# One core, a hybrid decoder trunk: attention values half a product later, one output block summed from PSUM, mixers shifted, and the recurrence's scores for half of the columns

## What is computed

```
mod = silu(c) @ w_ada + b_ada;  shift, scale, gate = split(mod)
h = rmsnorm(x, g_pre) * (1 + scale) + shift
p = h @ w_in                                   # 2048 x 1024 @ 1024 x 8704
y_pool = pool_mixer(a_in) * silu(a_g)
y_hgrn = hgrn2_mixer(b_q, b_f, b_i) * silu(b_g)   # gated linear recurrence, 4 heads of 64
y_conv = short_conv_mixer(c_x, c_b, c_c) * silu(c_g)
y_diff = diff_attention(d_q, d_k, d_v) * silu(d_g)  # a = softmax 0 - lambda * softmax 1, causal
merged = sum of sigmoid(m_g[branch]) * (y_branch @ w_merge[branch])
x + gate * rmsnorm(merged @ w_out, g_post)
```

## Time and profile before

| | us |
|---|---|
| median of 3 runs | 2758.57 |
| lowest, highest | 2758.25, 2764.52 |
| the profiled execution, as timed | 2759.86 |
| its span in the trace | 2757.8 |

### The profile page before, as it was taken

How to read it: one execution, slowest core, us unless ns; L and a number is a source line. 1 busy time by engine, 2 the same in 40 slices (tenths; PEclk the granted TensorE clock), 3 DMA queues, 4 the chain that set the end, 5 groups by cost and what they waited for, 6 DMA issues and landing times. The chain is left out here.

```text
span 2757.8 us, 35490 instructions
## 1 busy us (share of the span) xinstructions
PE 2355.1 (85%) x11572; PEld 1913.1 (69%) x11572; DVE 1773.7 (64%) x2868; ACT 1240.0 (45%) x2613; POOL 1231.3 (45%) x1015
## 2 busy tenths in 40 slices
PE   3698868778988889996899999998898965798898
PEld 3576656667776678785787777777677754677676
DVE  6775554544989896544777776688899734453442
ACT  3553444434443444543565656553444333243342
POOL 1442322222866665532333433465767605352543
PEclk9899988989999999998999999999999987899999
DMA  5357533323434334545342332143333356485772
GB/s 209 111 186 228 145 105 90 102 72 116 126 101 122 103 97 128 174 132 151 83 119 77 98 96 83 60 134 117 107 110 123 96 171 159 120 231 143 193 198 73
DMA packets 327262, 350.84 MB, mean 127 GB/s; under 512 B 26416, under 2 KB 244912, under 8 KB 326064
## 3 DMA queue, kind: packets, MB, share of 16 engines
q1 hardware_dynamic: 327088, 348.67, 42.8%
HBM read 242.15 MB, written 106.43 MB: 126 GB/s over the span
## 5 line engine op out<-in xcount | busy, mean ns | idle before, releaser
L1603 PE MATMUL gb<-h_hi,w_hi 128*128 128x512 f32 x1904 | 804.2, 422 | 83.7 <-DVE o L1199 53.4
L1604 PE MATMUL gb<-h_lo,w_hi 128*128 128x512 f32 x1904 | 766.9, 403 | 0.0
L1605 PE MATMUL gb<-h_hi,w_lo 128*128 128x512 f32 x1904 | 766.5, 403 | 0.0
L1191 DVE TENSOR_TENSOR w_lo<-w,w_hi 128x512 fp32r<-128x512 f32 x340 | 333.8, 984 | 337.3 <-ACT w_hi L900 336.5
L1603 PEld LDWEIGHTS gb<-h_hi,w_hi 128*128 128x128 f32 x1904 | 375.0, 197 | 173.7 <-issue 95.9
L1605 PEld LDWEIGHTS gb<-h_hi,w_lo 128*128 128x128 f32 x1904 | 372.4, 196 | 84.1
L1604 PEld LDWEIGHTS gb<-h_lo,w_hi 128*128 128x128 f32 x1904 | 375.4, 197 | 69.8 <-issue 0.2
L916 ACT ACTIVATE o<-gb 128x512 f32<-128x512 f32 x340 | 201.7, 593 | 347.8 <-PE gb L1605 300.1
L764 POOL TENSOR_TENSOR C_prob<-C_prob,C_cf 128x512 f32<-128x512 f32 (+3 forms) x160 | 157.8, 1006 | 383.8 <-DVE C_cf L1299 366.8
L989 ACT ACTIVATE C_prob<-C_sc,C_negm 128x512 f32<-128x512 f32 (+3 forms) x320 | 196.9, 620 | 280.9 <-DVE C_negm L1277 275.0
L748 POOL TENSOR_TENSOR o<-o 128x512 f32<-128x512 f32 x68 | 98.0, 1441 | 409.2 <-ACT o L916 409.1
(11 more groups left out here) (227 smaller groups left out, 4312.2 us busy)
## 6 DMA issues: line engine op xcount, KB each, us to landing
w<-in_w_in_dram SPq DMA_DIRECT2D x136, 512.0 KB, 4.1
gT_scratch<-o SPq DMA_DIRECT2D x128, 256.0 KB, 2.7
D_gate<-gT_scratch SPq DMA_DIRECT2D x32, 1024.0 KB, 9.6
pT_scratch<-o SPq DMA_DIRECT2D x80, 256.0 KB, 3.3
C_qt<-qB_scratch SPq DMA_DIRECT2D x128, 128.0 KB, 2.7
C_ks<-kT_scratch SPq DMA_DIRECT2D x48, 256.0 KB, 4.8
A_x_all<-in_x_dram SPq DMA_DIRECT2D x16, 512.0 KB, 6.5
A_ada<-in_w_ada_dram SPq DMA_DIRECT2D x8, 1024.0 KB, 12.1
```

Of the source, the lines that this page charges most:

```text
L1191: tt(w_lo[n % RING][:, :, :], source(n), w_hi[n % RING][:, :, :].bitcast(F32), ALU.subtract).then_inc(wlo, 1)
L1603: mm(to, hi[:, k, :], h_hi[j][:, k, :], start=(fresh and k == 0), stop=False, skip_group_check=True)
L1604: mm(to, hi[:, k, :], h_lo[j][:, k, :], start=False, stop=False, skip_group_check=True)
L1605: last = mm(to, lo[:, k, :], h_hi[j][:, k, :], start=False, stop=(k == KH - 1), skip_group_check=True)
```

## The change

- `ATTENTION` is `((50, 60), (284, 71))`: half 0 starts 12 slots earlier and takes 60 slots instead of 50; half 1 starts 3 slots earlier and takes 71.
- In half 0 the values, the transposes of the weights and the transpose back come half a product behind the scores on PE; the transpose back comes one piece earlier in the order (lag `ON` = 7), and DVE makes `y_out` ahead of the maxima. In half 1 PE's order stays; DVE makes `y_out` ahead of the combination, and ACT copies `at` between the two exponentials.
- Block 2 is summed by DVE straight from PSUM (`add_out` for j = 4); POOL's `cross` and ACT's copy of j = 4 go.
- The mixers of half 1 stand every 12.5 slots from 372 on; transposes, tokens, norms, root and finish move by one or two slots.
- The recurrence's scores of the 7 levels are made and picked for the 64 later columns alone. The diagonal reads `k_s` and `q_s` directly; POOL's two copies for it go. Scaling `k_s` and `f_s` moves from DVE to ACT.
- k and q of the first heads are made ahead of v; the row of `mod` is summed in slots 6 to 35, with one buffer.
- `qB` in HBM is laid out in another order: q is stored in 2 DMAs of 128 partitions instead of 4 of 64.
- The loads that open an attention half are spread over five slots.

```diff
-PAIR_COLS = (28, 30, 32, 34, 24, 20, 26, 22) + ...
+PAIR_COLS = (24, 20, 28, 30, 32, 34, 26, 22) + ...
+COPIED, SUMMED = (0, 2, 3, 6), (1, 4, 5)
-ATTENTION = ((62, 50), (287, 70))
-MIX_BASE = [130 + 12 * i for i in range(8)] + [374 + 12 * i for i in range(8)]
+ATTENTION = ((50, 60), (284, 71))
+MIX_BASE = [130 + 12 * i for i in range(8)] + [372 + 25 * i // 2 for i in range(8)]
-PREP, ROW = 5, 38
+PREP, ROW = 5, 6
...
+                y = 2 * at0 + s * 2 * span // att_steps[half]
+                att_at[divmod(y, 2)] = half, s
+                att_behind[divmod(y + 1 - half, 2)] = half, s
...
+                    to = qB[col - 20, t // P:t // P + 4].rearrange("b l m d t -> l (m d) b t")
+                    sp.dma_start(to[0], hb[x][:, :].rearrange("p (b t) -> p b t", t=P)).then_inc(hb_stored[x], 16)
+                    sp.dma_start(to[1], o[b][:, :].rearrange("p (b t) -> p b t", t=P)).then_inc(o_stored[b], 16)
...
+                    if 0 <= n - ATTENTION[half][0] + 5 < 5:
+                        begin_attention(half, n - ATTENTION[half][0] + 5)
...
-            def cross(u):
-                pool.wait_ge(copied, 5 * u + 4)
-                tt(o[2][:, :], o[2][:, :], o[3][:, :], ALU.add).then_inc(crossed, 1)
...
-                nc.gpsimd.tensor_copy(QX[:, t, NL - 1, :], q_s[i % 2][:, t, :])
-                nc.gpsimd.tensor_copy(X[:, t, NL - 1, :], k_s[i % 2][:, t, :]).then_inc(same, 1)
...
+                for t in range(2):
+                    a(f_s[:, t, :], f_s[:, t, :], ACT.Identity, scale=omlb[:, t:t + 1], bias=lb[:, t:t + 1])
+                    a(k_s[i % 2][:, t, :], k_s[i % 2][:, t, :], ACT.Copy, scale=omlb[:, t:t + 1])
...
+                    if new is not None:
+                        exps(new, 0)
+                    if turned_z is not None and half:
+                        copy_turned(turned_z)
+                    if new is not None:
+                        exps(new, 1)
...
-                b = {1: 0, 5: 1}[j]
+                b, c = {1: (0, 0), 4: (2, 3), 5: (1, 1)}[j]
...
+                tt(o[b][:, :], gb[n % 2][:, :], o[c][:, :], ALU.add).then_inc(summed, 1)
...
-                for t in range(2):
-                    ts(k_s[i % 2][:, t, :], k_s[i % 2][:, t, :], omlb[:, t:t + 1], None, ALU.mult)
-                for t in range(2):
-                    ins = ts(f_s[:, t, :], f_s[:, t, :], omlb[:, t:t + 1], lb[:, t:t + 1], ALU.mult, ALU.add)
...
+                        ins = nc.vector.copy_predicated(
+                            AT[:, r // 2, :, :].rearrange("p h (n u) -> p h n u", u=2 * m)[:, :, :, m:],
+                            later(masks[:, level, :], level).unsqueeze(1).to_broadcast([P, 2, P // (2 * m), m]),
+                            score[r % 2][:, :, y, 0:P // 2].rearrange("p h (n u) -> p h n u", u=m))
...
+                    i = None if half else finished(half, s, GATE)
+                    if i is not None:
+                        gate_out(i)
...
+                        if level < NL - 1:
+                            last = mm(later_packed(score[r % 2][:, h, y, :], level), X[rows_h, t, level, :],
+                                      later(QX[rows_h, t, level, :], level), start=True, stop=True)
+                        else:
+                            last = mm(score[r % 2][:, h, y, :], k_s[i % 2][rows_h, t, :], q_s[i % 2][rows_h, t, :], start=True, stop=True)
...
-                i = mix_step(n, 11)
+                i = mix_step(n, 12)
                 if i is not None:
                     norms(i)
```

251 lines of the change are left out of this document (127 added, 124 removed).

## The result

The changed kernel takes 2596.66 us (median of 4 runs, 2595.32 to 2598.16); the kernel before, run beside it, 2758.41. The ratio is 0.9409, 95% interval 0.9393 to 0.9426. The profiled execution took 2595.32 us, its span is 2593.5.

What follows compares the result with a forecast made beforehand. Limits: half 0's attention no full engine, PE waiting for DVE's gated output; mixers DVE nearest full; half 1's attention PE fullest. Terms -60, -16, -16, -20.5, -8 sum to -120.5 from a 2757.8 us span: forecast 2640, range 2600 to 2700.

Steps and rivals of the forecast that it cites:

- Attention of half 0, -60: Attention of half 0: waits of 76.8 us go, 11 and 6 come back, so 60 us less; bounds -25 and -85.
- -10.2: Start of attention of half 0: PE's 10.2 us wait for ACT goes, with opening loads spread and half as many q stores.
- the bound of -85: Attention of half 0: 85 us less if PE's granted clock of 0.87 also comes near half 1's 0.96.
- the loop's +11: Attention of half 0: `y_out`, 0.34 us, stands 32 times ahead of the maxima in DVE and ACT's hand-over, 11 us more.
- the +6 for the splittings: Attention of half 0: eight splittings of the q unit and k unit's end join DVE and ACT's hand-over, 6 us more.
- Attention of half 1, -20.5: Attention of half 1: opening pause -16.5, half-clock restart -2, ACT's copy of `at` -5, k unit +3; 20.5 us less.
- the bound of -35: Attention of half 1: at most 35 us less, if all 14.8 us of PE's wait for ACT's copy of `at` go.
- The mixers, -16 in each: Mixers of each half: DVE's net -23.8 counted one to one as -24, new PE wait +8; bounds -35 and +5.
- More is given back: Rival, chance 0.13: clock, POOL's port and the norms' wait give more in attention of half 0 and mixers; 2577, likely 2600.
- The loop did not take the holes: Rival, chance 0.17: DVE and ACT in turns bound attention of half 0, which gives -25 instead of -60; 2675 us.
- DVE's sums were not late: Rival, chance 0.12: half columns no cheaper and DVE's evictions late, so the mixers give nothing; 2672 us.
- the slower mechanism: Rival, chance 0.04: in the mixers DVE's new sum for j = 4 queues behind long operations, 5.07 us each; 2789 us.

Runs made afterwards that it cites:

- The spare addition: Changed kernel plus one 128x512 POOL addition at the head of its slot 5 in both attentions, 15 times, on a tile nobody waits for: 2594.84 us (0.941).

## Why the prediction was partly right

**Direction, stages and the main waits of the attentions: right.** The 66.6 us for `y_out`, most of the opening pauses and of the wait for `C_at` are gone, preparation gave 5.4 for 8, the untouched stages stood still.

**The step that failed: what counts as off the path.** "POOL loses 16.6 additions of 1.44 us per half and 32 copies in all; it is not on the path." So the sum had no gain for taking block 2 off POOL, and this edit, made alone, gives 64 us (2757.01 to 2692.72). Additions that nobody waits for do cost nothing in the attentions. But the addition for block 2 was a wait in POOL's queue, with the weights' sums behind it; it doubled the low part of the weights that DVE made beside it; and the copy was a piece of ACT's time and the release of a PSUM bank. Of these the queue's order is shown at about 13 us in attention of half 1; how the rest divides is open. The earlier trace rows had the sign of it: 409 us of idle time of POOL ahead of L748, which I read as spare time. The edit made alone is worth 12 us in attention of half 0, 23 in attention of half 1, 16 and 12 in the mixers; I had put it at 0, 0 and at a loss of 19 in each of the mixers (+11.3 for DVE's sum, +8 for PE's new wait). That loss did not come: in the kernel before with this edit (641 to 1066 us) PE waits for DVE's sums less than it did:

```profile
PE gb L1599 <- DVE o L1190: 10.4, 7, 2.7
```

against 16.8 us in eight.

**Attention of half 0, -60: the terms.** -66.6 and -10.2 were right as waits, though the loads' spreading was not what removed the 10.2. Between the same products PE stood idle for 84.7 us before and 30.9 now, 53.8 less, where the sum's -60 was all idle time. The other 28.2 us are PE's own work: 1460 matmuls took 304.8 us at a granted clock of 0.87, 1467 take 276.6 at 0.98. That is the missing 22: the sum had nothing for the clock, which stood in the bound of -85 alone, and the stage is near that bound. That the idle time came out near the forecast is partly luck. "60 slots for the same 57 steps means only that fewer steps share a slot" was costed at nothing and is worth 19 us (some 8 of PE's work, 11 of its idle time), and block 2 another 12. Against these stands a wait that the sum did not have, 26.2 us for `C_on`; of the loop's +11 6.5 showed, of the +6 for the splittings nothing was separated.

**Attention of half 1, -20.5: a term is missing.** Pause -12.6 instead of -16.5, copy about -6 instead of -5: near, the second in part by luck, since the copy's place mostly moved a wait of PE to another one. Block 2 alone gives the missing -23, part of it as idle time and part as a clock of 0.98 instead of 0.96, and -39.9 lies outside the bound of -35.

**The mixers, -16 in each: near in size (-14.6 and -23.4) by luck, for wrong reasons.** The sum had -15.0 for the picks (0 to 3 measured, since the picks did become 110 ns shorter each but DVE was not the limit), -20.1 for the scaling (8 and 4), +19.3 for block 2 (it alone gave -16 and -12). "In a stage where DVE is 84% busy I take this one to one" is the step that failed here: a share of 84% is no proof of a limit. In half 0 the edit for block 2 in the kernel before reaches 435.5 us, the whole changed kernel 437.0, though undoing the scaling costs it 8.2. What takes that back is open: undoing the halved scores (435.0) or the table of half 0 (438.2) moves the stage by 2 us or less, and the shifted norms were not tried. In half 1 "the 12.5 slots between blocks only spread them" was costed at nothing; with the table of half 1 it is worth 7 over both stages.

**The rivals.** "More is given back" was the nearest (2600 as a likely place), and of its three causes two are there. The clock is, as told above. POOL slowing DVE is: the forecast had put a fifth of each addition's length, 5 us in each half, and the one edit in the kernel before gave DVE 17 and 19 us of its other work back in the two mixers, where the prediction gave 24 as the most; but the time of these stages did not follow DVE's busy time, so it is not shown that this gave them their 16 and 12 us. The wait for `S` went in the changed kernel and was replaced. The loop did not take the holes, DVE's sums were not late, and nothing of the slower mechanism showed: a sum from PSUM takes 0.686 us, and PE waits for such sums 1.6 us each in ten.

## What to carry to other kernels

An instruction that waits in an in-order queue can cost what stands behind it, whatever its own length: where an engine sits idle for long in front of a cheap operation, look at what is queued behind that operation and who needs it, before calling the engine off the path. Look also at what the neighbour does at the same moment: a spare operation prices a length only if it runs beside the same work as the operation that it stands for. A busy share, even 84%, names a candidate for the limit; it is confirmed only if the stage's time moves with it, and a kernel with more work on that engine in the same time, as here 348 us busy against 335 by one edit, speaks against it. In a hand-made interleaving the number of steps that share a slot is a quantity of its own, worth 19 us here for ten slots and 6 more for four. And where the pauses of PE went, as in attention of half 0, its granted clock rose from 0.87 to 0.98 as well; what that gave back, 28 of the 82 us, belongs into the sum and not into the bound alone.

## What the runs showed of the hardware

A predicated copy from PSUM takes 340 ns for 128 columns of output and 450 for 256, so half of the columns is three quarters of the time. DVE's subtraction of 128x512, both inputs in SBUF, takes 690 ns with POOL idle and 1345 while POOL adds two 128x512 tiles (kernel before, 63 cases). The spare addition beside DVE's maxima of 512 columns, which read PSUM, did not lengthen them (675 ns against 680). The copy of 128x512 on ACT takes 0.63 us and cost the stage less than its length, 4.1 us for nine of them or fewer than half a us each. Scaling 128x128 by one value for each partition takes 388 ns on ACT in the changed kernel and 498 on DVE in the one with the scaling on DVE.
